# Two blocks of a transformer in split fp32 on one core: VectorE's low weights between the additions and the taps, ScalarE's silu one chunk later

## The reference, cut to what matters

```
u = h @ w_up                      # 1024 -> 2 x 2752
u = depthwise causal conv of width 3 (taps conv_w) + conv_b
gate, val = split(u)
x = x + (silu(gate) * val) @ w_down
```

## Time and profile before

| what | value |
|---|---|
| median of 3 runs | 1472.02 us (1471.1 to 1474.34) |
| the profiled execution | 1476.22 us, its span 1474.6 us |
| TensorE busy | 1463.2 us (99%) |
| VectorE busy | 1112.1 us (75%) |
| ScalarE busy | 940.5 us (64%) |
| GpSimd busy | 460.4 us (31%) |
| granted TensorE clock, mean | 0.998 of full speed |

### The profile page before, as it was taken

How to read it: one execution, slowest core, us unless ns; L and a number is a source line. 1 busy time by engine, 2 the same in 40 slices (tenths; PEclk the granted TensorE clock), 3 DMA queues, 4 the chain that set the end, 5 groups by cost and what they waited for, 6 DMA issues and landing times.

```text
span 1474.6 us, 25226 instructions
## 1 busy us (share of the span) xinstructions
PE 1463.2 (99%) x9928; PEld 1329.8 (90%) x9928; DVE 1112.1 (75%) x1877; ACT 940.5 (64%) x1600; POOL 460.4 (31%) x533
## 2 busy tenths in 40 slices
PE   8999999999999999999999999999999999999998
PEld 7999888899998888989888899998888999988888
DVE  6778899566478985786898666688986688797655
ACT  6776677457767774576677446766774568566453
POOL 2003366211133653211365321023553271022100
PEclk9999999999999999999999999999999999999999
DMA  7544565544335555471565545535655554355560
GB/s 269 184 154 150 188 226 203 197 162 152 144 117 200 204 198 199 167 232 58 200 215 204 196 170 180 178 119 199 222 203 185 173 206 180 110 209 200 177 221 34
DMA packets 39685, 264.98 MB, mean 180 GB/s; under 512 B 5247, under 2 KB 5562, under 8 KB 8976
## 3 DMA queue, kind: packets, MB, share of 16 engines
q1 hardware_dynamic: 36432, 255.54, 48.5%
q0 software_dynamic: 2992, 7.79, 2.2%
q10 hardware_dynamic: 144, 0.05, 0.0%
HBM read 262.24 MB, written 1.12 MB: 179 GB/s over the span
## 4 chain that ended last, share of the span: by engine, by line
PE 88%; DVE 6%; DMA 3%; ACT 2%; issue 1%; SPq 0%; POOL 0%; ACTq 0%; DVEq 0%
PE bank L1825 32%; PE bank L1822 16%; PE bank L1810 9%; PE bank L1811 8%; PE bank L1812 8%; PE bank L1873 5%; DVE w_lo L972 3%; PE bank L1882 2%; DMA w_raw<-w_std 2%; DVE tmp L1565 2%; PE bank L2057 1%; PE bank L2046 1%; PE bank L2038 1%; PE bank L2037 1%; PE bank L2417 1%
## 5 line engine op out<-in xcount | busy, mean ns | idle before, releaser
L972 DVE TENSOR_TENSOR w_lo<-w_raw,w_hi 128x2048 fp32r<-128x2048 f32 x239 | 550.1, 2309 | 74.5 <-ACT w_hi L425 74.4
L425 ACT CAST w_hi<-w_raw 128x2048 fp32r<-128x2048 f32 x239 | 453.3, 1905 | 47.8 <-DMA w_raw<-w_std 27.6
L1825 PE MATMUL bank<-h_both,w_hi 128*128 128x512 f32 x1472 | 462.3, 395 | 0.0
L1822 PEld LDWEIGHTS bank<-h_both,w_lo 128*128 128x128 f32 x1472 | 275.8, 188 | 68.4 <-DVE w_lo L972 3.2
L1822 PE MATMUL bank<-h_both,w_lo 128*128 128x256 f32 x1472 | 289.7, 278 | 1.8 <-DVE w_lo L972 1.4
L1825 PE MATMUL bank<-act_both,w_hi 128*128 128x512 f32 x848 | 267.4, 395 | 0.0
L1825 PEld LDWEIGHTS bank<-h_both,w_hi 128*128 128x128 f32 x1472 | 224.1, 189 | 0.0
L1822 PEld LDWEIGHTS bank<-act_both,w_lo 128*128 128x128 f32 x848 | 157.2, 188 | 34.2
L1780 POOL TENSOR_TENSOR tmp<-tmp 128x256 f32<-128x256 f32 x72 | 129.0, 1792 | 164.7 <-ACT tmp L909 164.7
L1822 PE MATMUL bank<-act_both,w_lo 128*128 128x256 f32 x848 | 170.1, 278 | 0.0
L1565 DVE SCALAR_TENSOR_TENSOR tmp<-bank,par,tmp 128x255 f32<-128x255 f32 (+1 forms) x306 | 131.6, 478 | 22.0 <-ACT tmp L905 21.9
(11 more groups left out here) (238 smaller groups left out, 2709.7 us busy)
## 6 DMA issues: line engine op xcount, KB each, us to landing
w_raw<-w_std SPq DMA_DIRECT2D x239, 1024.0 KB, 4.8
act_both<-vec_dram POOLq DMA_DIRECT2D x56, 128.0 KB, 3.4
w_raw<-w_std SPq DMA_DIRECT2D x3, 512.0 KB, 9.3
x<-xT SPq DMA_DIRECT2D x2, 512.0 KB, 6.0
out<-x SPq DMA_DIRECT2D x3, 256.0 KB, 2.2
w_raw<-w_std SPq DMA_DIRECT2D x2, 256.0 KB, 5.7
par<-params SPq DMA_DIRECT2D x1, 446.0 KB, 8.1
cst<-consts SPq DMA_DIRECT2D x1, 256.0 KB, 9.4
```

Of the source, the lines that this page charges most:

```text
L425: act.copy(w_hi[:, n % SLOTS, :], w_raw[:, n % RAW, :]).then_inc(hi_ready, 1)
L972: dve.tensor_tensor(w_lo[:, n % SLOTS, :], w_raw[:, n % RAW, :], w_hi[:, n % SLOTS, :].bitcast(F32), ALU.subtract).then_inc(lo_ready, 1)
L1822: pe.matmul(bank[:, 0:S], weights[k][1], moving[k][0], start=start and k == 0, stop=False, skip_group_check=True)
L1825: done = pe.matmul(bank[:, :], weights[k][0], moving[k][1], start=False, stop=stop and k == len(weights) - 1, skip_group_check=True)
```

## The change

In wide chunks of layers 0 to 3, VectorE calls `split()` right behind the additions of the halves and ahead of the taps; in all others it stays behind the taps. ScalarE no longer makes a wide chunk's silu in that chunk's step: it notes it in `silu_behind` and makes it in the next chunk's step, behind the copies of the second halves and ahead of the convolution starts (for chunk 20, at the start of `half_step`). No instruction is added or dropped.

```diff
--- before.py
+++ after.py
@@ -863,8 +863,18 @@
                 elif kind == "up":
                     convs = 2 if ffn < 4 else 1
 
+                    silu_behind = []
+
+                    def gate_behind():
+
+                        if silu_behind:
+                            j_, slot_ = silu_behind.pop()
+                            act.wait_ge(conv_part, j_ * 3 + (ffn * FT * 3 + 3))
+                            act.activation(cgate[:, slot_, :], cgate[:, slot_, :], ACT.Silu).then_inc(gated, 1)
+
                     def half_step(j, c, slot):
 
+                        gate_behind()
                         act.wait_ge(used, c + 1)
                         act.wait_ge(act_free, j + ffn * FT + 1)
                         at = j * 8 + PARAM["conv"] + ffn * FT * 8
@@ -905,6 +916,9 @@
                             act.activation(to[:, slot, :], source, ACT.Identity,
                                            bias=col(3), scale=col(2)).then_inc(conv_init, 1)
                         split()
+                        if wide and ffn < 4:
+                            silu_behind.append((j, slot))
+                            return
                         act.wait_ge(conv_part, (j * 3 + (ffn * FT * 3 + 3)) if ffn < 4 else (j * 2 + (4 * FT * 3 + 2)))
                         act.activation(cgate[:, slot, :], cgate[:, slot, :],
                                        ACT.Silu if ffn < 4 else ACT.Gelu_apprx_tanh).then_inc(gated, 1)
@@ -1555,6 +1569,9 @@
                                     dve.tensor_tensor(u_sb[:, 2 * (j % 2) + v, :], bank[slot][:, 0:S], to[:, slot, :],
                                                       ALU.add).then_inc(bank_free if v else half_added, 1)
 
+                            if ffn < 4:
+                                split()
+
                         def source(v):
                             if first or (wide and ffn == 4):
                                 return u_sb[:, 2 * (j % 2) + v, :]
@@ -1575,9 +1592,9 @@
                         if convs == 2:
                             dve.wait_ge(conv_part, part + 2)
                             tap(1, 2).then_inc(bank_free, 1)
-                        split()
                         if convs == 2 and wide:
                             return
+                        split()
                         dve.wait_ge(gated, n_ + 1)
                         if convs == 2:
                             dve.wait_ge(bank_free, c + (RING + 1))
```

## The result

| kernel | median | lowest to highest | profiled execution | its span |
|---|---|---|---|---|
| before | 1471.91 us | 1471.1 to 1479.1, 6 runs | 1476.22 us | 1474.6 us |
| changed | 1485.61 us | 1484.6 to 1486.1, 6 runs | 1484.68 us | 1483.1 us |

The ratio is 1.0083, with a 95% interval of 1.0071 to 1.0096. Between the medians the changed kernel is slower by 13.7 us (1.0093), where 8.2 us were forecast; the ratio is smaller since it goes by the means, and one run of before took 1479.1 us. The sign and the place were right; the size was not, and 1485.6 lies above the range.

The account below looks back on a forecast made before the run. TensorE, busy 1463.2 of 1474.6 us, was taken as the bound. Later chunk 7 starts less layer 0's second stall (5.9) plus GpSimd collisions (2.3) gave 8.2 us on the median 1472.02: 1480.2 us, range 1473.8 to 1483.2.

Parts of the forecast that it names:

- Step 4's low tiles ahead of the taps: VectorE makes low tiles 7 and 8 before chunk 4's taps, starting chunk 7 1.58 to 1.60 us later per layer.
- chunk 7 released by a tap: In layers 0 to 3, chunk 7 waits for chunk 4's last tap, no longer w_lo; 1.58 to 1.60 us later.
- no stall at chunk 9: Layer 0's second TensorE stall, at the start of chunk 9, goes; 0.5 us gained.
- 5.9 + 0.5 + 2.3: Layers 0 to 3: later chunk 7 starts net of layer 0's removed stall, 5.9; that stall, 0.5; GpSimd collisions, 2.3 us.
- The race for the port: Step 4: GpSimd's product starts before low tile 7, costing 0.58 us per layer; rival VectorE first, 5.9 us total, chance 0.33.
- GpSimd's next instruction gets no gap before the taps: Step 4: low tile 8 stands right behind 7, so no second GpSimd collision was counted.
- 5.9 + 2.3 = 8.2 us: Whole kernel: 5.9 us from later chunk 7 starts less layer 0's second stall, 2.3 from GpSimd collisions; chance 0.38.
- further stalls: Rival: a second stall at chunk 6 or 8 adds 2 to 4 us, giving 1483.5 us; chance 0.10.
- The base: Whole kernel: forecast counted from the runs' median, 1472.02 us, 4.2 below the profiled execution.
- The covers: Slack hiding other delays: 0.8 us at chunk 6, at least 0.7 at chunk 8, about 2 at the down stage.

Follow-up runs that it names:

- GpSimd was held back: Against before: the whole change, with GpSimd's product of chunk 3 waiting for the first tap of chunk 4; 1480.52 us, ratio 1.0055.
- the kernel with the clock kept: Against before: the whole change plus ten extra 512-column TensorE matmuls in place of the chunk 7 stall in four layers; 1481.27 us, ratio 1.0062.
- a lead of three: Against before: the whole change, with VectorE making low weights three ahead throughout the wide chunks; 1486.7 us, ratio 1.0097.

## Why the prediction was right and wrong

- **The mechanism and its place were right.** Step 4's low tiles ahead of the taps; chunk 7 released by a tap; once in each of four layers; no stall at chunk 9. Chunk 7 of layer 0 was due near 171.1, and 167.04 with the 4.17 us of the earlier start is 171.2. The other kernels that move or remove the extra tile confirm it.
- **The length of the stall was nearly right.** From additions to taps 6.80 us and 0.58 were counted; it took 7.49 (159.41 to 166.90). The idle time of the w_lo matmuls rose by 8.8 us, where 6 to 8 were forecast. Chunk 3 to chunk 7 grew by 9.1 us in all where 8.7 (5.9 + 0.5 + 2.3) were forecast.
- **The race for the port went as taken**: GpSimd first, by 0.04 us. The statement "GpSimd's next instruction gets no gap before the taps" failed. The cast fell in with the second tile, which took 2.48 us and not 2.28, and cost another 0.19 us a layer. The Trainium skill ("SBUF — State Buffer", who interferes with whom) lets issue order decide, and the cast was issued ahead of the second tile: the trace agrees, with 5.25 us for the pair, and 4.48 once GpSimd was held back.
- **The step that failed is the sum**: "5.9 + 2.3 = 8.2 us" has no term for TensorE's clock. It holds the time at which chunk 7 starts, and takes for granted that the matmuls behind it run as fast as ever. The mean granted clock of before, 0.998, seems to allow that, and in the up stages before had no stall over about half a us. But the trace of before had the price elsewhere: the one stall of that length, 2.73 us ahead of 35.46, was followed by the clock of 0.51 and cost some 1.4 us on top. Four such stalls would have added 5.6 us, by an estimate from that price. The missing term is 4.2 us by the trace and 4.3 by the kernel with the clock kept. With it the sum would have been 12.4 us, 1484.4. Of the Trainium skill, "TensorE: Matmul & The Clock Gate", section "HAM oscillation — how this bites in real kernels", bears on it: waits between stretches of work can send the array back to the slower clock, paid again at each. The waits of its example are of 3 to 5 us. Here 2.62 to 2.70 us were enough in three of four layers, so the drop should have been a rival.
- **The range was too narrow for the same reason**: its top, 1483.2, was built from further stalls, not from the price of one.
- **The base was right.** Going from the median and not from the profiled 1476.22 us was taken to be worth 4.2 us. That is the wait at the start that the profiled execution alone had, with the slow stretch behind it. The prediction gives no reason for the difference.
- **The covers** at chunks 6 and 8 and at the down stage held in the changed kernel. The other kernels show how thin they are: a stall of 1.8 us at chunk 8 once chunk 4 keeps the old order, and of 2.4 to 2.9 us at the down stage once one weight is missing.

## What to carry to other kernels

When work is put ahead of an instruction that frees a buffer, look for the one step in which that work comes twice; the steady step says nothing about it, and moving the doubled piece within the step only picks another victim. A stall of 2 to 3 us on a TensorE that is otherwise busy should be priced with what it may cost behind it: here 9.4 us of stalls brought 4.3 us of slower clock. Look for a stall of that length anywhere in the trace before; here it stood in the first 40 us, in a part that the change doesn't touch. Where two halves of an edit can be built alone, build them: here one gained 1.5 and 1.6 us in two runs, and the other lost 12.4.

## What the runs showed of the hardware

- The lower clock (0.50 of the full one) does not go by the length of the stall alone. It came behind the stalls of 2.62, 2.70 and 2.68 us of the changed kernel and not behind that of 2.60; with the silu in its old place, behind 2.80 and 2.91 us (layers 2 and 3) and not behind 2.87 and 2.86; with a lead of three, behind 2.55, 2.38 and 2.88 us and not behind 2.44; with GpSimd held back, behind 1.87, 1.82 and 1.87 us and not behind 1.80; and never behind the four of 1.75 to 1.77 us at chunk 8. What decides it is open. A kernel with such stalls varies from run to run: the six runs of the changed kernel have mean granted clocks of 0.995 to 0.997, and the two with 0.995 are the slowest (1486.1 and 1486.0 us).
- VectorE's low tile, two SBUF inputs, and GpSimd's instructions that read SBUF hold each other up in both directions: the tile goes from 2.28 to 2.85 us behind a product, and GpSimd's cast from 0.40 to 2.34 us behind a tile. By its booked end, 0.33 us behind the start of the second tile, a cast that waits gets its turn between two tiles issued back to back.
